# Retention: values of all heads first by seven half-size products, two heads at a time; a head's transposes between q and k of the next head

## The reference, cut to what matters

```
proj = u @ w_qkvg                                  # q 1024, k 1024, v 2048, g 2048 columns
q, k = rotary(q), rotary(k)                        # per head
o    = chunked retention of q, k, v with decay     # in the kernel: (q k^T * decay) v
o    = (o - mean) * rsqrt(var + eps) * gn_w        # per head and token
out  = (silu(g) * o) @ w_o
```

## Time and profile before

| what | value |
|---|---|
| median of 3 runs | 1252.6 us (1251.73 to 1252.9) |
| the profiled execution's own time | 1253.15 us |
| its span, first to last instruction | 1251.3 us |
| mean granted TensorE clock in it | 0.998 |
| PE busy | 1216.0 us, 97% of the span |
| DVE busy | 856.7 us, 68% |
| ACT busy | 532.2 us, 43% |

### The profile page before, as it was taken

The page is one execution under the profiler, slowest core; times in us unless marked ns, Lnnn a source line. Parts: engine busy times, 40 slices in busy tenths (PEclk is TensorE's granted clock), DMA queues, the critical chain, the costliest instruction groups (busy, mean ns, idle before and its releaser), DMA issues.

```text
span 1251.3 us, 18814 instructions
## 1 busy us (share of the span) xinstructions
PE 1216.0 (97%) x7693; PEld 1067.7 (85%) x7693; DVE 856.7 (68%) x1009; ACT 532.2 (43%) x693; POOL 64.5 (5%) x84
## 2 busy tenths in 40 slices
PE   3889999999999999999999999999999999999997
PEld 3778889889988998888888888888889889988986
DVE  8997778578857868746655466544388578757866
ACT  5655465335533545333343333422355235523543
POOL 5950000000000000000000000000000000000000
PEclk9999999999999999999999999999999999999999
DMA  5653232423332333323232132323333323333321
GB/s 118 155 110 118 84 118 73 130 68 102 111 125 68 105 98 119 109 68 110 68 100 80 62 109 71 97 67 101 101 101 100 103 85 113 107 102 91 104 76 68
DMA packets 166521, 121.89 MB, mean 97 GB/s; under 512 B 6104, under 2 KB 158736, under 8 KB 166416
## 3 DMA queue, kind: packets, MB, share of 16 engines
q1 hardware_dynamic: 164784, 118.24, 31.4%
q10 hardware_dynamic: 1664, 2.62, 1.0%
HBM read 114.29 MB, written 2.10 MB: 93 GB/s over the span
## 4 chain that ended last, share of the span: by engine, by line
PE 93%; POOL 3%; DVE 1%; ACTq 1%; ACT 1%; issue 0%; DMA 0%; SPq 0%; DVEq 0%; POOLq 0%
PE bank L820 18%; PE bank L821 17%; PE bank L822 17%; PE bank L877 9%; PE bank L876 9%; PE bank L875 9%; PE bank L1004 2%; PE bank L1003 2%; PE bank L1002 2%; ACTq L518 1%; PE bank L1030 1%; PE bank L1032 1%; PE bank L1031 1%; PE bank L716 1%; PE bank L1041 1%; POOL s_pool_tmp L2147 1%
## 5 line engine op out<-in xcount | busy, mean ns | idle before, releaser
L1095 ACT ACTIVATE w_hi<-w_raw 128x2048 fp32r<-128x2048 f32 (+1 forms) x70 | 130.5, 1864 | 193.4 <-PE bank L822 174.6
L820 PE MATMUL bank<-u_hi,w_hi 128*128 128x512 f32 x480 | 188.2, 392 | 0.0
L822 PE MATMUL bank<-u_hi,w_lo 128*128 128x512 f32 x480 | 186.8, 389 | 0.0
L821 PE MATMUL bank<-u_lo,w_hi 128*128 128x512 f32 x480 | 186.8, 389 | 0.0
L1511 DVE TENSOR_TENSOR w_lo<-w_raw,w_hi 128x2048 fp32r<-128x2048 f32 x46 | 105.4, 2291 | 65.8 <-ACT w_hi L1095 65.8
L1501 DVE TENSOR_TENSOR tmp<-bank,tmp 128x512 f32<-128x512 f32 (+2 forms) x118 | 77.8, 659 | 89.3 <-PE bank L822 54.2
L875 PE MATMUL bank<-s_hi,w_hi 128*128 128x256 f32 x408 | 115.5, 283 | 0.0
L876 PE MATMUL bank<-s_lo,w_hi 128*128 128x256 f32 x408 | 115.5, 283 | 0.0
L877 PE MATMUL bank<-s_hi,w_lo 128*128 128x256 f32 x408 | 115.5, 283 | 0.0
L820 PE MATMUL bank<-hid_hi,w_hi 128*128 128x512 f32 x288 | 113.0, 392 | 0.9 <-issue 0.9
L822 PE MATMUL bank<-hid_hi,w_lo 128*128 128x512 f32 x288 | 112.2, 389 | 0.0
(11 more groups left out here) (274 smaller groups left out, 2737.3 us busy)
## 6 DMA issues: line engine op xcount, KB each, us to landing
w_raw<-in_ret_w_qkvg_dram SPq DMA_DIRECT2D x24, 1024.0 KB, 5.0
w_raw<-in_ffn_w_up_dram SPq DMA_DIRECT2D x44, 512.0 KB, 3.7
w_raw<-in_ffn_w_gate_dram SPq DMA_DIRECT2D x44, 512.0 KB, 4.8
w_raw<-in_ffn_w_down_dram SPq DMA_DIRECT2D x16, 1024.0 KB, 5.0
w_raw<-in_ret_w_o_dram SPq DMA_DIRECT2D x8, 1024.0 KB, 5.2
w_raw<-in_ffn_w_down_dram SPq DMA_DIRECT2D x8, 768.0 KB, 4.4
w_raw<-in_s_glu_w_dram SPq DMA_DIRECT2D x4, 1024.0 KB, 5.1
s<-in_x_dram ACTq DMA_DIRECT2D x8, 256.0 KB, 8.7
```

Of the source, the lines that this page charges most:

```text
L820: pe.matmul(o, w_hi[w][:, w_cols], hi, start=first, stop=False)
L821: pe.matmul(o, w_hi[w][:, w_cols], lo, start=False, stop=False)
L822: return pe.matmul(o, w_lo[w][:, w_cols], hi, start=False, stop=end)
L1095: return act.activation(o, i, ACT.Copy, scale=scale)
```

## The change

The values of all heads come first. After q and k of head 0 (whose raw results ACT copies out to `q_raw`), v is made for two heads at a time as one product of a 512 x 1024 matrix u by a 1024 x 1024 weight block, cut into halves in all three directions and done by Strassen's scheme in Winograd's form: seven products of half-size instead of eight, each 24 products of 128 x 512 on PE (`v_block`). The seven are named by the weight block they use: B11, B21, B22 as loaded, T1 to T4 made by DVE as differences of blocks (T1 = B12 - B11, T2 = B22 - T1, T3 = B22 - B12, T4 = B21 - T2). u's sums (`us_raw`, split into `us_hi`, `us_lo`) are made once, before the first product. Partial results are carried on in PSUM: ACT copies a finished bank into another one (`v_seed`) and PE goes on adding there. Finished values go to `v_raw` in SBUF by ACT (`v_out`) or DVE (`v_added`).

In each head the q and k of the next head then stand on both sides of the transposes of this one, and the loops over heads are written out. The first two tiles of `wo` are interleaved: 12 steps of tile 0, the last head's transposes, 8 steps of tile 1, the rest of tile 0, the rest of tile 1. Everything from the second pair of `wo` tiles on stands as before. The core of the diff (PE, then ACT, then DVE):

```diff
-PAIRS = {"glu": 2, "ffn0": len(UNITS) // 2, "ret": 12, "wo": 4, "ffn1": len(UNITS) // 2}
+PAIRS = {"glu": 2, "ffn0": len(UNITS) // 2, "ret": 15, "wo": 4, "ffn1": len(UNITS) // 2}
+V_BLOCKS = ["B11", "B21", "T1", "T2", "T3", "B22", "T4"]
...
+            def v_block(p, name):
+                s, pair = v_unit(p, name)
...
+                pe.wait_ge(w_lo_ready[s], pair + 1)
+                for t in range(2):
+                    b = banks[t]
+                    if name == "B11":
+                        open_bank(b, v_free(b, p))
+                    elif name == "T1":
+                        open_bank(b, v_free(b, 2 * p))
+                    else:
+                        pe.wait_ge(v_seeded[t], seeds)
+                    for k in range(KH):
...
+                        pe.matmul(o, a_hi, w_hi[s][:, cols], start=fresh and k == 0, stop=False, skip_group_check=True)
+                        pe.matmul(o, a_hi, w_lo[s][:, cols], start=False, stop=False, skip_group_check=True)
+                        mm = pe.matmul(o, a_lo, w_hi[s][:, cols], start=False, stop=end, skip_group_check=True)
+                    if t == 0:
+                        mm.then_inc(v_done, 1)
+                mm.then_inc(w_used[s], 1)
...
+            def head(h):
+                if h:
+                    two_tiles(0, qk_pair(h), [4, 5], [ret_free(b, 2 * h - 1) for b in (4, 5)], None, 0)
+                    turned(h - 1)
+                    two_tiles(1, qk_pair(h), [6, 7], [ret_free(b, 2 * h - 1) for b in (6, 7)], None, 0)
+                two_tiles(0, g_pair(h), [4, 5], [ret_free(b, 2 * h) for b in (4, 5)], None, 0)
...
+                if s == 0:
+                    wo_part(0, 0, range(0, 12))
+                    turned(H - 1)
+            wo_part(0, 1, range(0, 8))
+            wo_part(0, 0, range(12, 16)).then_inc(w_used[0], 1)
+            wo_part(0, 1, range(8, 16)).then_inc(w_used[1], 1)
...
+            v_sums_high(2)
+            v_sums_high(3)
+            v_high(0, "B11")
             root(1)
             root_columns(6, "norm1")
+            raw_out(0)
+            for p in range(V_PAIRS):
+                for name in V_BLOCKS:
+                    follows = v_next(p, name)
+                    if follows:
+                        v_high(*follows)
...
+                    for t in range(2):
+                        if name in ("B11", "T2", "T3"):
+                            v_seed(p, name, t)
+                        elif name in ("B21", "T1", "T4"):
+                            v_out(p, name, t)
...
+            for k in range(KH):
+                v_sums(k)
+                if k:
+                    v_sums_low(k - 1)
+            v_sum(0, "T1")
+            v_sums_low(KH - 1)
             inverse_rms(1)
+            v_low(0, "B11")
             inverse_columns(6, "norm1", 1)
...
+            for p in range(V_PAIRS):
+                for name in V_BLOCKS:
+                    follows = v_next(p, name)
+                    if follows:
+                        v_low(*follows)
+                    else:
+                        split_weights(0, g_pair(0))
+                    made = {"B21": "T2", "T1": "T3", "T2": "T4"}.get(name)
+                    if made:
+                        v_sum(p, made)
```

More of the change, by code:

```diff
@@ L366, in trunk @@
         ret.close()
+        q_raw = tmp[:, 0:4, :]
+        v_p5 = [tmp[:, 4 + t, :] for t in range(2)]
+        b11 = qk[:, :, :].rearrange("p t a -> p (t a)")
+        b12 = o_norm[:, :, :].rearrange("p t a -> p (t a)")
+        b21 = gate[:, :, :].rearrange("p t a -> p (t a)")
+        b22, t12 = w_raw[:, 0, :], w_raw[:, 1, :]
+        v_weights = {"B11": b11, "B12": b12, "B21": b21, "B22": b22, "T1": t12, "T2": t12, "T3": b12, "T4": b21}
         last = ExitStack()
@@ L434, in trunk @@
         seeded = [sem(f"seeded{s}") for s in range(2)]
+        v_loaded = {name: sem(f"v_loaded_{name}") for name in ("B11", "B12", "B21", "B22")}
+        vt_ready = sem("vt_ready")
+        v_done = sem("v_done")
+        v_seeded = [sem(f"v_seeded{t}") for t in range(2)]
+        v_split = sem("v_split")
         a_ready = sem("a_ready")
@@ new lines, in _ @@
+            ret0 = PAIR0["ret"]
+            load_unit(0, ret0, ret_v[:, :, 0:HD], KT, HD)
+            load_unit(1, ret0, ret_v[:, :, D:D + HD], KT, HD)
+            for name in ("B11", "B21", "B12"):
+                load_v(0, name)
+            sp.wait_ge(w_lo_ready[0], ret0 + 1)
+            load_v(0, "B22")
+            for p in range(1, V_PAIRS):
+                before = 4 * (p - 1)
+                for name, user, made in (("B11", "B11", 1), ("B12", "T3", 3), ("B22", "B22", 3), ("B21", "T4", 4)):
+                    s, pair = v_unit(p - 1, user)
+                    sp.wait_ge(w_lo_ready[s], pair + 1)
+                    sp.wait_ge(vt_ready, before + made)
+                    load_v(p, name)
@@ L980, in _ @@
             chunked_products(0, 0)
[L983 to L1007, removed]
@@ L1033, in head @@
+                        pe.matmul(o, c_hi, y_hi[:, 4 * h + jt, :], start=False, stop=False)
+                        mm = pe.matmul(o, c_lo, v_hi[:, jt, :], start=False, stop=(jt == it))
                     mm.then_inc(bank_full[it], 1)
[L1034 to L1042, removed]
@@ L1048, in _ @@
+            wo_part(0, 1, range(0, 8))
+            wo_part(0, 0, range(12, 16)).then_inc(w_used[0], 1)
+            wo_part(0, 1, range(8, 16)).then_inc(w_used[1], 1)
+            with pe.Fori(1, KT // 2) as i:
                 for s in range(2):
                     pe.wait_ge(w_lo_ready[s], i + PAIR0["wo"] + 1)
[L1050 to L1054, removed]
@@ new lines, in v_full, with v_seed @@
+            def v_full(p, name, t):
+                s, pair = v_unit(p, name)
+                if t:
+                    act.wait_ge(w_used[s], pair + 1)
+                else:
+                    act.wait_ge(v_done, len(V_BLOCKS) * p + V_BLOCKS.index(name) + 1)
+            def v_seed(p, name, t):
+                into = {"B11": V_X, "T2": V_Y, "T3": V_W}[name][t]
+                v_full(p, name, t)
+                act.wait_ge(bank_free[into], v_free(into, 2 * p + 1 if name == "T3" else p))
+                copy(bank[into][:, :], bank[V_Z[t]][:, :]).then_inc(v_seeded[t], 1)
@@ L1435, in _ @@
[L1435 to L1451, removed]
-                act.wait_ge(bank_free[3], free[3] + 2)
-                copy(scores_hi[:, :], scores_raw).then_inc(scores_hi_ready, 1)
-                split_weights(1, pair + 2)
-                split_weights(0, pair + 3)
-                for m in range(2):
-                    silu_gate(free, m)
```

453 lines of the change are left out of this document (336 added, 117 removed).

## The result

| what | before | after |
|---|---|---|
| median of 10 runs each | 1252.69 us (1251.39 to 1253.91) | 1254.9 us (1253.62 to 1256.66) |
| ratio after to before | | 1.0019, 95% interval 1.0011 to 1.0027 |
| profiled execution's own time, span | 1253.15 us, 1251.3 us | 1253.81 us, 1252.0 us |
| mean granted TensorE clock in it | 0.998 | 0.997 |

The change costs 2.2 us. The ratio's interval leaves out 1, so the kernel is a little slower, but by less than the 0.2% that the prediction takes for no change; it is 1.3 us above the forecast. 48 products were saved, and all of their time was given back.

The account below looks back on a forecast made before the run. PE, busy for 97% of the span, was taken as the bound: 1253.15 - 10.88 + 5.8 + 1.3 + 3.6 + 1.2 = 1254.2 us, forecast as a median of 1253.6 us, range 1249.7 to 1257.0.

Parts of the forecast that it names:

- The saving: Value products: 336 instead of 4 x 96, 48 fewer on PE, 10.88 us saved.
- The start: Start of retention: PE waits for B11's low part, behind the sums and reciprocal in DVE's queue; +5.8 us.
- the first rival: Start of retention costs nothing: DVE is through before PE finishes k, no pause or half clock; 1246.5 us, 13%.
- T2 and T3: Within the seven value products: PE waits 0.75 us at T2 and 1.05 at T3; +3.6 us for four heads.
- the second rival: Value products: T2 and T3 do not wait, because preparation runs further ahead after the long pause; 1250.0 us, 11%.
- The output projection: Slot 0's next weights take 6.6 us against 5.44 us of cover from tile 1's remainder; +1.2 us, once.
- Nothing in the heads: Heads after the values: PE work covers DVE's turning of q and k and the normalization; no waits, no cost.
- The clock: Behind the pause at retention's start, PE's clock falls to half speed for 3.4 us; +1.3 us.
- The third rival: After the pause, half clock lasts for twice 3.4 us of work, costing 3.4 us; 1255.7 us, deciding from 2.8 us, 22%.
- That the time stays the same: Whole kernel: saving given back in waits, median 1253.6 us; same means 1250.1 to 1255.1 us, chance 0.55.

Follow-up runs that it names:

- e6: Kernel after with e1, e2 and e3 combined, the reciprocal taken in two halves behind T3's and B22's low parts; 1241.61 us, ratio 0.9914 to before.
- e7: e6 plus 24 products with unused results behind each of the two sevens, so PE has as many products as before; 1251.9 us, ratio 1.0000.
- e1: Kernel after with B11's high and low parts earlier in the queues, the reciprocal and the rotary table's scaling later; 1247.14 us, ratio 0.9955.
- e2: Kernel after with T2 made in B11's place, so the sums of T2, T3 and T4 come one product earlier; 1251.71 us, ratio 0.9995.
- e3: Kernel after with output projection tile 1 doing 6 steps instead of 8 ahead of the rest of tile 0; 1253.67 us, ratio 1.0007.
- e5: Kernel after with a head's transposes ahead of the next head's q instead of between q and k; 1274.06 us, one run.
- e4: Kernel after with 24 products of unused result filling PE's pause ahead of the first value product; 1252.55 us, ratio 1.0003.

## Why the prediction was right, and where it was off

- **The saving** of 10.88 us is right: 48 products fewer on the page, 11.1 us in e6, 10.3 us in e7.
- **The start** (5.8 us) is right with its mechanism. The wait measured 5.9 us by its row and 6.04 from start to start. The steps fit too: the reciprocal's end was forecast 3.5 us behind PE's end of k (518.8 against 515.26) and came 3.65 behind (517.73 against 514.08), and it is DVE's queue and ACT's root together that set it, as worked out. e1 shows it: another place in the queue, and the wait is gone. So the first rival fails for the order as written; it is the case of e1, at 1247.1 us where it was priced at 1246.5.
- **T2 and T3** (3.6 us) are right with their mechanism: 2.3 us of waits, 3.3 us with the late products behind them, 3.2 us in e2, so the second rival fails too. T2's wait was forecast at 0.75 us and is 0.57 from start to start (0.42 by its row), T3's at 1.05 and is 0.88 (0.72). The copy from bank to bank, which had no row, was taken at 0.65 us; it has 0.58, and ACT's next instruction starts 0.49 behind it (527.29 to 527.78):

```profile
L1234 ACT ACTIVATE bank<-bank 128x512 f32<-128x512 f32 x12 | 7.0, 582 | 20.3 <-PE bank L1117 20.3
```

- **The output projection** (1.2 us) is right: 1.28 us by its row, 1.45 from start to start, 1.2 us in e3.
- **Nothing in the heads** is right: no wait there, and e5 shows what the cover is worth.
- **The clock** (1.3 us) is the one term that was clearly mis-sized. The mechanism held, and e4 shows it. The size came from one stretch of 3.4 us, and here the half clock stood for 6.8 us in each of the four profiled executions with this pause (after, e2, e3 and e5); only how much of it met work differs. In after 3.0 us of work fell in it, in e2 3.1, in e3 6.2 and in e5 5.7. At half clock a product takes 0.43 us instead of 0.2267, so of each us of such work 0.47 is lost: 1.4, 1.5, 2.9 and 2.7 us, 2.1 in the mean, which agrees with e4's 2.0 to 2.4. The third rival was to decide from 2.8 us on, and two of the four lie there or next to it.

- **That the time stays the same** came out by little. 1254.9 us lies 0.2 us under the 1255.1 from which the prediction calls a kernel slower, and three of the ten runs lie above it. The mechanism was right; that a clock term which was too small still gave the right side was in part luck.

The sum with the measured terms is 1252.7 - 10.9 + 6.0 + 2.1 + 3.3 + 1.5 = 1254.7 us, against 1254.9 measured.

## What to carry to other kernels

When work is taken from the bounding engine, ask what prepares its next unit and how long that takes against the new, shorter unit: 10.9 us saved on PE were given back in waits and half clock, more than half of it at one place, because work that PE did not yet need stood ahead of the one operation that it needed next. Of the 21 new operations there e1 left 19 where they were; to pass the last two and the reciprocal was enough. An engine that is idle for more than a quarter of the span (DVE, busy for 72%) can still be late at one place, and then order, not load, is to be mended: give the queue in the order in which the bounding engine needs things, and move what nobody awaits (here a reciprocal) to where there is room. A pause of PE can cost more than its own length: in the four executions with the pause of 5.9 us the granted clock fell while PE stood still and came back only after 3.0 to 6.2 us of work.

## What the runs showed of the hardware

The price of the half clock differs between executions. Behind one and the same pause 6.8 us of it met 3.0 us of PE's work in after and 6.2 us in e3. The Trainium skill, "TensorE: Matmul & The Clock Gate" (Part 1: The HAM clock gate), says of the start of a kernel that the number of products at half speed differs from run to run in one and the same kernel; the 7 and 15 products in the windows of after and e3 agree, though these are two kernels with the same start. So such a term is a spread to be put into the range, not one number.

A run's mean granted clock does not measure that price, since the same 6.8 us lower it by the same amount whatever they meet. Ten runs of after lie 3 us apart; the four with a mean of 0.997 have 1253.62 to 1254.9 us, the three with 0.995 1254.96 to 1256.66. But in the profiled executions the difference between 0.997 (after) and 0.995 (e2, e3) is another 3.4 us of half clock far ahead of the change: the granted clock is 0.59 in the mean from 56 to 60 us in e2 and 0.57 from 79 to 83 us in e3, and in after it is 1.00 from 40 to 500 us. How much of the 3 us belongs to which stretch is not shown.

A pause need not be long: in e5 a wait of 2.6 us, with some tenths more between the transposes behind it, was followed by the same 6.8 us of half clock as the wait of 5.9 us in after, and there it lay on PE's work for nearly all of its time. Behind the same wait in the two other heads it stood for 3.4 us.
